# Block 1's half of the modulation summed on VectorE, in PSUM, inside the feed-forward

## The reference, cut to what matters

```python
# block 1, for each of 2 layers
z = rmsnorm(x, mix_norm) @ w_in            # RG-LRU, latent attention (MLA), forgetting attention (FoX), gates
merged = g0 * y_lru + g1 * y_mla + g2 * y_fox
x = x + merged @ w_o
hf = rmsnorm(x, ffn_norm) @ w_gate_up      # 1024 -> 2 x 2816
x = x + (silu(hf[:, :2816]) * hf[:, 2816:]) @ w_down
x = x + sigmoid(rmsnorm(x, ple_norm) @ w_ple_gate) * (p @ w_ple)
# block 2, for layers i = 0 (pooling) and 1 (attention), on the latents x and on a context of 256 tokens
sh1, sc1, g1, sh2, sc2, g2 = split(silu(c) @ ada_w[i] + ada_b[i], 6)     # and the same with c_ctx
h = h + g1 * mix(modulate(rms_norm(h), sh1, sc1))
h = h + g2 * (relu(modulate(rms_norm(h), sh2, sc2) @ w1) ** 2 @ w2)
```

## Time and profile before

| | before |
|---|---|
| median of 3 runs | 1848.58 us (1848.19 to 1850.12) |
| the profiled execution, time | 1850.33 us |
| its span | 1848.5 us |
| busy: PE, POOL, DVE, ACT | 94%, 64%, 50%, 48% |
| chain that ended last, share of PE | 77% |
| TensorE clock granted, mean | 0.978 |
| read from HBM | 295.89 MB, 161 GB/s over the span |

### The profile page before, as it was taken

The page is one execution under the profiler, slowest core; times in us unless marked ns, Lnnn a source line. Parts: engine busy times, 40 slices in busy tenths (PEclk is TensorE's granted clock), DMA queues, the critical chain, the costliest instruction groups (busy, mean ns, idle before and its releaser), DMA issues.

```text
span 1848.5 us, 32240 instructions
## 1 busy us (share of the span) xinstructions
PE 1745.9 (94%) x12690; PEld 1607.1 (87%) x12690; DVE 926.0 (50%) x2042; ACT 888.0 (48%) x1462; POOL 1176.7 (64%) x768
## 2 busy tenths in 40 slices
PE   7899999999999899999999969999999979989997
PEld 6888899999999778999999958888888768689997
DVE  6678435313366784353233666854444585642223
ACT  6535546445666346455445864232323353554443
POOL 6876678788878766677788723444444443158884
PEclk9999999999999999999999989999999999999999
DMA  6543365665555434656655503454453521035552
GB/s 236 196 135 119 128 222 200 220 217 184 178 188 192 146 115 137 218 209 207 219 189 174 198 27 126 145 185 176 154 182 137 182 92 60 33 108 190 182 183 81
DMA packets 83414, 299.02 MB, mean 162 GB/s; under 512 B 9152, under 2 KB 11456, under 8 KB 83008
## 3 DMA queue, kind: packets, MB, share of 16 engines
q1 hardware_dynamic: 81648, 294.02, 46.9%
q10 hardware_dynamic: 1616, 2.95, 0.5%
HBM read 295.89 MB, written 1.05 MB: 161 GB/s over the span
## 4 chain that ended last, share of the span: by engine, by line
PE 77%; DVE 9%; POOL 4%; ACT 3%; issue 3%; DVEq 2%; DMA 1%; ACTq 0%; SPq 0%
PE bank L978 23%; PE bank L982 23%; PE bank L981 23%; POOL wlo L927 4%; PE bank L992 1%; DMA raw<-in_stream 1%; PE bank L1250 1%; ACT whi L1397 1%; PE bank L1158 1%; DVE split_acts L1855 1%; PE bank L1174 1%; PE bank L1221 1%; DVE acts L2098 1%; PE bank L1144 1%; DVE acts L2139 1%
## 5 line engine op out<-in xcount | busy, mean ns | idle before, releaser
L927 POOL TENSOR_TENSOR wlo<-raw,whi 128x256 fp32r<-128x256 f32 (+1 forms) x756 | 1171.0, 1573 | 650.8 <-ACT whi L1397 650.0
L978 PE MATMUL bank<-split_acts,whi 128*128 128x256 f32 (+1 forms) x3492 | 1061.2, 304 | 27.1 <-DVE split_acts L1855 16.7
L981 PE MATMUL bank<-split_acts,whi 128*128 128x256 f32 (+1 forms) x3492 | 1048.5, 300 | 0.0
L982 PE MATMUL bank<-split_acts,wlo 128*128 128x256 f32 (+1 forms) x3492 | 1048.4, 300 | 0.0
L1397 ACT ACTIVATE whi<-raw 128x1024 fp32r<-128x1024 f32 x459 | 483.0, 1055 | 545.7 <-DMA raw<-in_stream 306.3
L978 PEld LDWEIGHTS bank<-split_acts,whi 128*128 128x128 f32 x3492 | 671.9, 192 | 69.0 <-issue 27.5
L981 PEld LDWEIGHTS bank<-split_acts,whi 128*128 128x128 f32 x3492 | 672.6, 193 | 20.7
L982 PEld LDWEIGHTS bank<-split_acts,wlo 128*128 128x128 f32 x3492 | 672.0, 192 | 21.2
L1855 DVE TENSOR_TENSOR split_acts<-bank,split_acts 128x256 fp32r<-128x256 f32 (+1 forms) x212 | 97.9, 462 | 51.2 <-ACT split_acts L1541 20.0
L2524 DVE SCALAR_TENSOR_TENSOR acts<-bank,acts 128x256 f32<-128x256 f32 x104 | 47.4, 481 | 149.7 <-PE bank L982 149.3
L1903 DVE SCALAR_TENSOR_TENSOR acts<-raw,acts 128x512 f32<-128x512 f32 x112 | 113.6, 1035 | 8.5 <-issue 2.9
(11 more groups left out here) (280 smaller groups left out, 1645.5 us busy)
## 6 DMA issues: line engine op xcount, KB each, us to landing
raw<-in_stream SPq DMA_DIRECT2D x555, 512.0 KB, 3.7
acts<-in_x SPq DMA_DIRECT2D x1, 1024.0 KB, 6.4
acts<-in_ctx ACTq DMA_DIRECT2D x1, 1024.0 KB, 6.9
acts<-in_const ACTq DMA_DIRECT2D x1, 1024.0 KB, 5.1
out<-acts SPq DMA_DIRECT2D x8, 128.0 KB, 2.1
acts<-in_const SPq DMA_DIRECT2D x1, 711.0 KB, 8.5
acts<-in_p ACTq DMA_DIRECT2D x2, 256.0 KB, 3.2
acts<-in_const ACTq DMA_DIRECT2D x1, 320.0 KB, 3.1
```

Of the source, the lines that this page charges most:

```text
L927: last = nc.gpsimd.tensor_tensor(wlo[slot][:, cols], raw[source][:, cols], whi[slot][:, cols].bitcast(F32), ALU.subtract)
L978: first = nc.tensor.matmul(out_ap, w_hi, hi_act(k), start=(k == 0), stop=False)
L981: nc.tensor.matmul(out_ap, w_hi, lo_act(k), start=False, stop=False)
L982: last = nc.tensor.matmul(out_ap, w_lo, hi_act(k), start=False, stop=(k == k_tiles - 1))
```

## The change

All 48 chunks of the modulation's first half go the way of the second: summed by DVE, now within block 1's feed-forward, and added over partitions by `sum` tiles on PE.

- The `ada` and `turn` tiles and their helpers go. In each layer 24 places get one chunk each: before `hg` 0,1 to 0,9, `dn` 0,1 to 0,6 and `hg` 1,0 to 1,8; six `sum` tiles follow.
- The running sum lies in PSUM (`mod_parts`, banks 6 and 7, one per side); the last k-step writes to SBUF, where PE reads it. Block 2's sums stay in SBUF.
- In the stream's order every such chunk, block 2's too, stands four tiles later than its place in DVE's order (`fetch_tiles`, `FETCH_BEHIND = 4`).
- `c_square` has two banks and no longer four; `opening_gains` moves from behind `dn` 0,7 to behind `hu` 1,5 of layer 1; PE no longer waits for `silu_ready` at the start.

```diff
+SUM_CHUNKS = 4
+SUM_BEHIND = 2
+def with_sums(tiles, places):
+    out, n, due = [], 0, []
+    for i, t in enumerate(tiles):
+        if due and due[0][1] <= i:
+            out.append(("sum", due.pop(0)[0]))
+        for _ in range(places.get(t, 0)):
+            out.append(("mod", n))
+            n += 1
+            if n % SUM_CHUNKS == 0:
+                due.append((n // SUM_CHUNKS - 1, i + SUM_BEHIND))
+        out.append(t)
...
+FETCH_BEHIND = 4
+def fetch_tiles(tiles):
+    out, late, i = [], [], 0
     for t in tiles:
+        if t[0] == "mod":
+            late.append((t, i + FETCH_BEHIND))
+            continue
+        while late and late[0][1] <= i:
+            out.append(late.pop(0)[0])
         out.append(t)
+        i += 1
+    return out + [t for t, _ in late]
...
-HEAD_TILES, _n = with_modulation(HEAD_TILES, {("u", 1): 1, ("gl", 0): 1, ("ss", "q"): 1, ("rotk", 0): 1},
-                                 0, flush=(("kn", 2),))
-MID_TILES, _n = with_modulation(MID_TILES, {("g", 2, 0): 1, ("g", 2, 2): 1, ("g", 2, 4): 1, ("g", 2, 6): 1}, _n,
-                                flush=(("y", 2, 7),))
-TAIL_TILES, _n = with_modulation(TAIL_TILES, {("hg", 0, 3): 1, ("hg", 0, 6): 1, ("hg", 0, 9): 1, ("dn", 0, 3): 1}, _n,
-                                 flush=(("dn", 0, 6),))
+FFN_PLACES = {**{("hg", 0, j): 1 for j in range(1, 10)}, **{("dn", 0, n): 1 for n in range(1, 7)},
+              **{("hg", 1, j): 1 for j in range(9)}}
+ALL_TAIL_TILES, LAYER_MODS = with_sums(TAIL_TILES, FFN_PLACES)
...
-ORDER, RAW_AT = chunk_plan(ALL_TILES, ALL_SPANS)
+ORDER, RAW_AT = chunk_plan(FETCH_TILES, ALL_SPANS)
...
-        c_square = [bank[4], bank[5], bank[6], bank[7]]
+        c_square = [bank[4], bank[5]]
+        mod_parts = [bank[6], bank[7]]
...
-            def modulation(b):
-
-                for part in range(ADA_CHUNKS):
-                    c, k = RAW_OF[("ada", Cursor.ada)], Cursor.ada % KT
-                    Cursor.ada += 1
-                    pe.wait_ge(raw_in[c % RING], (c // RING + 1) * 16)
-                    for strip in range(4):
-                        last = nc.tensor.matmul(b[32 * strip:32 * strip + 32, 0:256], silu_c[:, 2 * k:2 * k + 32],
-                                                raw[c % RING][:, strip * 256:(strip + 1) * 256],
-                                                start=(part == 0), stop=(part == ADA_CHUNKS - 1))
-                    last.then_inc(ada_used, 1)
-                return last
...
+            def sum_parts(b, half):
+
+                pe.wait_ge(mod_summed, half + 1)
+                for s in sum_of(half)[2]:
+                    for i in range(4):
+                        last = nc.tensor.matmul(b[:, 2 * i + s:2 * i + s + 1], tile(mod_sums[half % 2][s], i, P),
+                                                ones[:, 0:1], start=True, stop=True)
                 return last
...
-                if k >= 4:
-                    act.wait_ge(csq_used, k - 3)
+                if k >= 2:
+                    act.wait_ge(csq_used, k - 1)
...
                     for s in sides:
                         w, total = raw[c % RING][:, k % 2 * 512:(k % 2 + 1) * 512], mod_sums[half % 2][s]
+                        part = mod_parts[s][:, :] if n < DEPTH * LAYER_MODS else total
                         factor = silu_c[:, 2 * k + s:2 * k + s + 1]
                         if k == 0:
-                            last = v.tensor_scalar(total, w, factor, None, ALU.mult)
+                            last = v.tensor_scalar(part, w, factor, None, ALU.mult)
                         else:
-                            last = v.scalar_tensor_tensor(out=total, in0=w, scalar=factor, in1=total, op0=ALU.mult,
-                                                          op1=ALU.add)
+                            last = v.scalar_tensor_tensor(out=total if k == KT - 1 else part, in0=w, scalar=factor,
+                                                          in1=part, op0=ALU.mult, op1=ALU.add)
...
                     for m in BEFORE[t]:
-                        dve.wait_ge(gemm_done, lay * N_TILES + TILE_NO[m] + 1)
-                        take_modulation(m, bank[(lay * N_TILES + TILE_NO[m]) % N_BANKS], rows,
-                                        lay * LAYER_ADA // PLACES + m[1])
+                        if m[0] == "mod":
+                            modulation_sum(lay * LAYER_MODS + m[1])
+                        else:
+                            dve.wait_ge(gemm_done, lay * N_TILES + TILE_NO[m] + 1)
+                            take_sum(lay * LAYER_SUMS + m[1], bank[(lay * N_TILES + TILE_NO[m]) % N_BANKS])
...
                     for j in range(HALF_T):
                         of_tile(("hg", part, j))
                         of_tile(("hu", part, j))
+                        if (part, j) == (1, 5) and lay == DEPTH - 1:
+                            opening_gains()
...
-                    if part == 0 and lay == DEPTH - 1:
-                        opening_gains()
```

More of the change, by code:

```diff
@@ L80 @@
     + [("rotq", 0), ("rotq", 1)])
[L82 to L89, removed]
-    for t in tiles:
[L91 to L99, removed]
+SUM_CHUNKS = 4
[11 more added lines that the diff above has]
+        out.append(t)
+    assert not due
+    return out, n
+FETCH_BEHIND = 4
+def fetch_tiles(tiles):
+    out, late, i = [], [], 0
+    for t in tiles:
+        if t[0] == "mod":
[3 more added lines that the diff above has]
+            out.append(late.pop(0)[0])
         out.append(t)
-    assert turned * PLACES == n
-    return out, n
+        i += 1
+    return out + [t for t, _ in late]
 MLA_FILL = [("fl", 0)] + [("fq", j) for j in range(4)] + [("fk", j) for j in range(4)] + BRANCH_TILES[0][:7]
@@ L135, in modulation_before @@
     for t in tiles:
-        if t[0] in ("ada", "turn", "mod", "sum"):
+        if t[0] in ("mod", "sum"):
             run.append(t)
@@ L158 @@
 ATOM_SPAN, LAYER_ATOMS = first_atoms()
-ADA_CHUNKS = 2
-assert PLACES * ADA_CHUNKS == KT
 LEAD = 2
 def chunk_plan(tiles, spans):
-    order, at, adas, late, needed = [("split", n) for n in range(LEAD)], {}, 0, [], 0
-    runs = {"ada": ADA_CHUNKS, "mod": 1}
+    order, at, mods, late, needed = [("split", n) for n in range(LEAD)], {}, 0, [], 0
     splits = LEAD
     for t in tiles:
-        if t[1][0] in runs:
-            run = [("ada", adas + i) for i in range(runs[t[1][0]])]
-            adas += len(run)
+        if t[1][0] == "mod":
+            run = [("mod", mods)]
+            mods += 1
             if splits > needed:
@@ L201, in chunk_reach @@
             freed_by, m = order[r + 1 - RING] if r + 1 >= RING else ("split", 0)
-            if kind == "split" and (n >= needed + SLOTS_AHEAD or (freed_by == "ada" and m >= adas)):
+            if kind == "split" and (n >= needed + SLOTS_AHEAD or (freed_by == "mod" and m >= mods)):
                 break
             r += 1
-        reach[t] = r
+        reach[t], mods = r, placed
     return reach
@@ L255 @@
     + [("ss", 1, 1)] + mlp_tiles(1) + [("ss", "last")])
-SUM_CHUNKS = 4
-SUM_BEHIND = 2
-def with_sums(tiles, places):
-    out, n, due = [], 0, []
-    for i, t in enumerate(tiles):
-        if due and due[0][1] <= i:
-            out.append(("sum", due.pop(0)[0]))
-        for _ in range(places.get(t, 0)):
-            out.append(("mod", n))
-            n += 1
-            if n % SUM_CHUNKS == 0:
-                due.append((n // SUM_CHUNKS - 1, i + SUM_BEHIND))
-        out.append(t)
-    assert not due
-    return out, n
 MLP_PLACES = [((w, 0, q, j), 1) for q in range(QUARTERS)
@@ L481, in layer_atoms @@
     for t in TILES:
-        if t in SHARED or t[0] in ("ada", "turn"):
+        if t in SHARED or t[0] == "sum":
             continue
@@ L950, in _ @@
                 atom = 0
-                ada = 0
             def weights(n):
@@ L1038, in gemm @@
                     b = open_bank(t)
-                    if kind == "ada":
-                        modulation(b)
-                        pe.drain().then_inc(gemm_done, 1)
-                        return
-                    if kind == "turn":
-                        out_of_bank(("ada", PLACES * j + PLACES - 1))
-                        turn_rows(b, rows).then_inc(gemm_done, 1)
+                    if kind == "sum":
+                        sum_parts(b, lay * LAYER_SUMS + j).then_inc(gemm_done, 1)
                         return
@@ L1246, in gemm2 @@
                 elif kind == "sum":
-                    pe.wait_ge(mod_summed, t[1] + 1)
-                    for s in sum_of(t[1])[2]:
-                        for i in range(4):
-                            last = nc.tensor.matmul(b[:, 2 * i + s:2 * i + s + 1], tile(mod_sums[t[1] % 2][s], i, P),
-                                                    ones[:, 0:1], start=True, stop=True)
+                    last = sum_parts(b, DEPTH * LAYER_SUMS + t[1])
                 elif kind == "py":
@@ L2378, in _ @@
                 for t in MID_TILES:
-                    if t[0] not in ("ada", "turn"):
```

(2 more changed lines are left out.)

91 lines of the change are left out of this document (32 added, 59 removed).

## The result

Eighteen runs of each kernel: 1852.54 us after (1851.55 to 1854.85) against 1849.65 before (1846.68 to 1855.32). The ratio is 1.002, its 95% interval 1.0014 to 1.0027: slower, by 2.9 us in the medians and 3.7 by the ratio, where 5.7 us faster was forecast.

A forecast was written before the change was run, and what follows sets the result against it. PE was taken as the bound (busy 94%), POOL in layer 0's head. Branches -11.0, feed-forward +9.5, heads -1.5 and -3.7, stalls +1.0 gave -5.7 us: 1842.9 from 1848.58, range 1836.5 to 1853.

The forecast's parts named there:

- the last sentence on fetches: Moving `opening_gains` between two chunks in the feed-forward may make one `sum` wait 0.5 us, counted within the range.
- the sum's +1.0: Feed-forward: PE stalls waiting for DVE at the first sum of each gate run, +1.0 us, between 0 and 4.
- DVE's row of 0.75: Feed-forward chunks: each new 512-column DVE instruction with its sum in PSUM takes 0.75 us.
- Rivals A and B: DVE late at feed-forward sums, 1861 or 1879 (chance 0.14); PSUM dearer at 512 columns, 0.80 an instruction, 1848 (0.09).
- The balance at the sums: Feed-forward: over four gate/up pairs and a sum DVE needs 24.65 us, PE 24.75, so DVE keeps pace by 0.1.
- Sizes of what goes and comes: PE tiles: each `ada` frees 1.29 us, each `turn` 0.36, each new feed-forward `sum` costs 1.71.
- Heads: After `fv` the variance and reciprocal start sooner: -1.16 and -0.36 us in layer 0, -3.7 in layer 1.
- rival C: Heads do not give, ACT finds another split to wait for: net -1.8, 1846.8 us; chance 0.12.
- its two terms: Layer 0's head: -1.16 us for the earlier reciprocal and -0.36 for the `turn` behind it.
- Fetches at four tiles: SP's queue: modulation chunks placed four tiles late hold up nothing on PE, cost 0.
- rival D: Chunks too late in the down tiles, DVE then a `sum` waits: 6 to 12 us back, 1849 to 1855; chance 0.08.
- the terms of heads, branches and feed-forward: Heads -1.5 and -3.7 us, branches -11.0, feed-forward +9.5 from -11.0 removed and +20.5 for `sum` tiles.

The follow-up runs named there:

- e1: Changed kernel with `opening_gains` after the last gate/up pair (1,10) of layer 1, behind the last sum, instead of after (1,5): 1847.47 us.
- e2: Changed kernel with block 1's sums four tiles behind their last chunk instead of two, `opening_gains` left in place: 1843.67 us.
- e4: Changed kernel with the instructions of `opening_gains` also after the pair (1,5) of layer 0: 1858.89 us.
- e8: Changed kernel with the four `norm_gains` instructions and a drain after (1,5) of layer 1, the rest of `opening_gains` after (1,10): 1846.9 us.
- e6: Changed kernel with block 1's running sums in SBUF instead of in two PSUM banks: 1988.46 us.
- e3: Kernel before, with only `opening_gains` moved to the changed kernel's place, after the pair (1,5) of layer 1: 1850.47 us.
- e9: Changed kernel with 24 extra products on PE just ahead of the last sum of layer 1, their result overwritten: 1850.55 us.
- e7: e2 with every modulation chunk fetched at DVE's own place in the stream instead of four tiles later: 2026.94 us.

## Why the prediction was wrong, step by step

- **The step that failed** is the last sentence on fetches: "`opening_gains` moves between two chunks and may make one `sum` wait 0.5: in the range". It measured a gap of 3.04 us in place of 0.5, and 3.1 us for the clock that had no term: 6.0 in all (changed kernel against e1). Of DVE's 3.2 us the instructions themselves are 0.8; the rest is the wait for POOL, which the sentence did not count. Shown from four sides: away (e1), with slack (e2), in both layers (e4), and a part of it (e8). It could have been priced. The trace of before has the step, again with a wait for POOL in it (POOL's low part ran 931.25 to 933.65):

```profile
932.30 1.61 DVE L2014 SCALAR_TENSOR_TENSOR acts<-acts 128x8 f32<-128x8 f32 x4
933.83 0.23 DVE L2022 TENSOR_TENSOR acts<-acts 128x8 f32<-128x8 f32 x2
934.14 0.17 DVE L2025 TENSOR_TENSOR acts<-acts 128x8 f32<-128x8 f32 x1
```

  2.0 us there, and my own balance for DVE over four pairs and a sum left 0.1. The two belonged in one sum: 2.0 to 3.2 late, all of it at the last `sum`.
- **The range.** 1852.54 lies just inside the stated 1836.5 to 1853, but only by the width that the rivals gave it, and through none of them: that it is inside is luck. The direction was wrong.
- **No term for the clock.** The plan counted idle time of PE at its length. Here a gap of 3 us cost 6, one of half a microsecond up to 2 (the changed kernel's gap at 872 with the 3.41 us of half clock behind it: 2.1 between chunks 240 and 248 against e1, which had neither). These make the 8.6: 6.0 + 2.1 + 0.5 for the first sum of layer 1, and only the last was in the sum's +1.0.
- **DVE's row of 0.75 was right:** 0.752 over 144 instructions, none above 0.759. Rivals A and B fall as they were put. By the Trainium skill (VectorE: DVE Perf Modes, The TRN2 errata — SBUF-src ops pay a fixed extra latency per instruction), cited there, the form with all in SBUF would be some 0.065 us shorter; the medians are 0.752 in SBUF (e6) and 0.754 in PSUM, and the measurement decides. (The 0.691 that the prediction set against the page had no SBUF row beside it and could not settle this.) Only a half's first step, a plain multiply (L1861), is shorter in SBUF: 0.487 us in block 2 against 0.750 into PSUM.
- **The balance at the sums was right:** the cycle is 5.81 to 5.88 instead of 6.05, and e1's last sum comes with 0.1 to spare. Apart from the last one of layer 1, three sums stalled, 0.86, 0.49 and 0.49, +1.8 in all against +1.0.
- **Sizes of what goes and comes:** an `ada` freed 1.39 rather than 1.29, since the first product after one is itself late; a `sum` cost 1.78 rather than 1.71; a `turn` 0.43. In the feed-forward these offset each other, 4.7 measured; the branches have no `sum`, and are 0.4 to 0.5 shorter than put.
- **Heads:** the chains start as worked out, and rival C falls. DVE in both heads, for the earlier trace rows:

```profile
83.05 1.75 DVE L2043 RECIPROCAL acts<-acts 128x256 f32<-128x256 f32 x1 [0.48 <-ACT acts L1460]
...
592.89 1.40 DVE L2247 TENSOR_SCALAR acts<-bank,acts 128x512 f32<-128x512 f32 x2
...
595.10 1.75 DVE L2043 RECIPROCAL acts<-acts 128x256 f32<-128x256 f32 x1 [0.48 <-ACT acts L1460]
```

  Layer 0: 83.05, 83.14 predicted. Layer 1: 595.10; layer 0 ended 2.64 earlier than before, so on the old time axis 597.74, 597.95 predicted, and the wait for ACT is 0.48 instead of 2.62. Layer 0's head gave 2.3 in all, 0.8 more than its two terms; where that comes from stays open.
- **Fetches at four tiles cost 0,** as put; rival D falls. But the margin is not as wide as the text lets one think: two tiles are free, none costs 183 us.

With e2's slack the terms of heads, branches and feed-forward stand to half a microsecond each, and it gives 1843.7 against the forecast 1842.9. That the two are so near is in part luck: e2 has no stalls, which the sum had at +1.0, and lost 1.3 us in the rest of the kernel, which it had at 0. The prediction read the change as twelve sums and some stalls; its sign was decided by seven instructions of 128x8.

## What to carry to other kernels

When an edit fills an engine to the brim, list everything else that the engine does in that stretch, tiny steps included, and price each with the wait for a shared port that it may meet; then give the consumer slack for the worst (here two tiles later, free) instead of cutting the room exact. Count a gap of some 3 us in a dense TensorE stage at twice its length, because the clock may fall behind it. In a queue that issues in order, ask whether the one who frees a late slot waits, over other engines, for what stands behind it in the queue.

## What the runs showed of the hardware that was not expected

- A 128x8 DVE instruction with both inputs in SBUF took 0.17 us free (e1, e3) and 2.24, 2.41 us (changed kernel, e4) beside a POOL instruction of 2.40: size gives no shelter.
- Half clock behind short gaps of PE: gap beyond the normal start 0.45 us, 3.41 us at half; 0.49, 3.41 or none; 0.86, 6.83, 3.41 (e9) or none; 2.9, 6.83 (changed kernel, e4); 3.6, 10.24 (e4). All of these stand ahead of a `sum`. A gap of 0.89 between two products at 510.17 us of the changed kernel had none behind it, and none in the other kernels either; but of the 22 gaps of 3 us and more in e7's feed-forwards, none of them ahead of a `sum`, 21 had half clock at or behind their end. Of 6.83 us at half, 3.1 were lost. The Trainium skill (TensorE: Matmul & The Clock Gate, Terms) puts the penalty at about the throttled time times the share of pulses withheld, an estimate of 3.4, a little above it.
- DVE's 512-column multiply-add takes 0.75 us with the running sum in PSUM and in SBUF alike; only POOL makes the difference, and it made 136 us of it, some 40 of them by the clock (e6 against the changed kernel).
